# One meeting of the engines per stage, two state recurrences run per feature tile, and a fifth attention term on 128 rows

## The reference

```python
def _hgrn_scan(state, ins, emit):            # chunk by chunk
    def step(S, inp):
        ...
            inter = jnp.einsum('bhtk,bhkv->bhtv', q_c * jnp.exp(g), S)
        ...
        S = (jnp.exp(g_last[:, :, 0, :])[..., None] * S
             + jnp.einsum('bhsk,bhsv->bhkv', k_c * jnp.exp(g_last - g), i_c))
        return S, o

def _rwkv_scan(state, ins, emit):            # token by token
    def step(S, inp):
        sa = jnp.einsum('bhvk,bhk->bhv', S, kk_t)
        S = (S * w_t[:, :, None, :] - sa[..., None] * (kk_t * a_t)[:, :, None, :]
             + v_t[..., None] * k_t[:, :, None, :])
        y = jnp.einsum('bhvk,bhk->bhv', S, inp[5]) if emit else None
        return S, y

def block_attention(qn, qr, kn, kr, v):      # 8 heads, 512 queries, 768 keys
        s = jnp.einsum('bqhd,bkhd->bhqk', qn_b, kn) + jnp.einsum('bqhd,bkd->bhqk', qr_b, kr)
        p = jax.nn.softmax(s.astype(jnp.float32) * scale, axis=-1).astype(v.dtype)
        return jnp.einsum('bhqk,bkhd->bqhd', p, v)
```

## Time and profile before

| what | us |
|---|---|
| median of 3 executions | 2939.48 (2936.7 to 2940.68) |
| the profiled execution | 2932.05 |
| its span, first to last instruction | 2930.1 |
| one pass of the hgrn state stage, first to last work | 9.6 |
| one pass of the rwkv state stage | 24.8 |
| the attention stage | 138 |
| granted TensorE clock, mean | 0.922 |

### The profile page before, as it was taken

The page is one execution under the profiler, slowest core; times in us unless marked ns, Lnnn a source line. Parts: engine busy times, 40 slices in busy tenths (PEclk is TensorE's granted clock), DMA queues, the critical chain, the costliest instruction groups (busy, mean ns, idle before and its releaser), DMA issues. The chain is left out here.

```text
span 2930.1 us, 60098 instructions
## 1 busy us (share of the span) xinstructions
PE 2539.1 (87%) x25174; PEld 2106.5 (72%) x25174; DVE 1476.8 (50%) x2524; ACT 905.7 (31%) x1456; POOL 618.6 (21%) x323
## 2 busy tenths in 40 slices
PE   6956597786977798978988899999997898899998
PEld 3845485684855587768887788888885765688886
DVE  6787777536437764345553444134315455643242
ACT  3243224213124432522124322122214433432232
POOL 0010200110113121200103223222341300544444
PEclk9977697896988899989999999999998999899999
DMA  6521061000005342200004112111214200523232
GB/s 267 180 80 45 14 205 42 3 4 1 4 3 215 138 157 86 72 28 3 3 3 151 51 64 71 58 57 64 71 44 180 77 1 16 200 100 99 89 104 82
DMA packets 63139, 229.31 MB, mean 78 GB/s; under 512 B 6352, under 2 KB 12880, under 8 KB 60880
## 3 DMA queue, kind: packets, MB, share of 16 engines
q1 hardware_dynamic: 62928, 226.22, 22.3%
HBM read 211.52 MB, written 13.63 MB: 77 GB/s over the span
## 5 line engine op out<-in xcount | busy, mean ns | idle before, releaser
L2323 POOL TENSOR_TENSOR b_wl<-b_stage,b_wh 128x1024 fp32r<-128x1024 f32 (+1 forms) x72 | 186.7, 2593 | 477.1 <-ACT b_wh L2319 477.1
L2622 DVE SCALAR_TENSOR_TENSOR f_xr<-f_ps,cols,f_xr 128x511 f32<-128x511 f32 (+1 forms) x132 | 83.2, 658 | 326.2 <-ACT f_xr L2615 326.2
L2454 PE MATMUL f_ps<-h_h,b_wl 128*128 128x256 f32 (+1 forms) x672 | 226.3, 337 | 0.0
L2454 PE MATMUL f_ps<-h_h,b_wh 128*128 128x256 f32 (+1 forms) x672 | 226.1, 336 | 0.0
L2454 PE MATMUL f_ps<-h_l,b_wh 128*128 128x256 f32 (+1 forms) x672 | 225.8, 336 | 0.0
L2319 ACT ACTIVATE b_wh<-b_stage 128x1024 fp32r<-128x1024 f32 (+1 forms) x72 | 81.5, 1131 | 460.3 <-PE f_ps L2454 404.9
L2323 POOL TENSOR_TENSOR c_wl<-c_stage,c_wh 128x1024 fp32r<-128x1024 f32 (+1 forms) x68 | 176.6, 2597 | 221.6 <-ACT c_wh L2319 221.6
L2319 ACT ACTIVATE c_wh<-c_stage 128x1024 fp32r<-128x1024 f32 (+1 forms) x68 | 77.3, 1137 | 266.3 <-PE f_ps L2454 232.8
L2323 POOL TENSOR_TENSOR a_wl<-a_stage,a_wh 128x1024 fp32r<-128x1024 f32 x33 | 85.2, 2581 | 269.2 <-ACT a_wh L2319 269.2
L2454 PEld LDWEIGHTS f_ps<-h_h,b_wh 128*128 128x128 f32 x672 | 127.6, 190 | 13.7
L2454 PEld LDWEIGHTS f_ps<-h_h,b_wl 128*128 128x128 f32 x672 | 127.6, 190 | 13.2
(11 more groups left out here) (716 smaller groups left out, 6698.0 us busy)
## 6 DMA issues: line engine op xcount, KB each, us to landing
b_stage<-in_ffn_up SPq DMA_DIRECT2D x44, 512.0 KB, 3.2
c_stage<-in_ffn_up SPq DMA_DIRECT2D x44, 512.0 KB, 3.2
first_stage<-in_w_in SPq DMA_DIRECT2D x33, 512.0 KB, 3.7
a_stage<-in_ab_w SPq DMA_DIRECT2D x25, 512.0 KB, 3.6
p_hgrn_side_w<-in_ada_w SPq DMA_DIRECT2D x12, 1024.0 KB, 5.0
b_stage<-in_ffn_down SPq DMA_DIRECT2D x16, 704.0 KB, 4.1
c_stage<-in_ffn_down SPq DMA_DIRECT2D x16, 704.0 KB, 4.1
a_in_side_w<-in_ada_w SPq DMA_DIRECT2D x8, 1024.0 KB, 6.4
```

What stands on the lines that cost most here:

```text
L2323: self.nc.gpsimd.tensor_tensor(self.wl[:, slot, :w], self.stage[:, slot, :w], self.wh[:, slot, :w].bitcast(F32), ALU.subtract).then_inc(se ...
L2454: done = self.nc.tensor.matmul(out[s][:, :tn], w, x[:, k, t0:t0 + tn], start=k == 0 and n == 0, stop=k == job.kt - 1 and n == 2)
L2622: nc.vector.scalar_tensor_tensor(out, b[:, :n - 1], self.tap(part, 0, i), out, ALU.mult, ALU.add).then_inc(self.before_ok[part], 1)
```

## The change

`Stage.__exit__` no longer holds the second meeting. The semaphores that a stage gives up are cleared by POOL behind the first meeting as before, but they are kept out of use during the next stage and are handed back only at its end:

```diff
     def __exit__(self, *exc):
         self.mem.close()
         if exc[0] is None:
+            for s in Stage.kept_back:
+                self.nc.release_semaphore(s)
             self.nc.clear_and_free_semaphores(self.sems)
-            self.nc.all_engine_barrier()
+            Stage.kept_back = [self.nc.alloc_semaphore(f"{s.name}_kept_back", num=s.num) for s in self.sems]
```

`hgrn_states` gives each feature tile its own semaphore and its own two banks; decay and addition become one operation:

```diff
-                nc.vector.tensor_tensor(tmp[:, :, :], states[:, c], spread(w["end"][:, :, c], 2, HD), ALU.mult
-                                        ).then_inc(decayed, 1)
-                dve.wait_ge(decayed, n + 2)
-                dve.wait_ge(update, n + 1)
-                nc.vector.tensor_tensor(states[:, order[n + 1]], tmp[:, :, :],
-                                        ps[n % 4][:, :NR * HD].rearrange("p (f v) -> p f v", v=HD), ALU.add
-                                        ).then_inc(added, 1)
+                for f in range(NR):
+                    dve.wait_ge(state_ok[f], n + 1)
+                    dve.wait_ge(update, NR * n + f + 1)
+                    nc.vector.scalar_tensor_tensor(states[:, order[n + 1], f], states[:, c, f], w["end"][:, f, c:c + 1],
+                                                   ps[f][n % 2][:, :HD], ALU.mult, ALU.add).then_inc(state_ok[f], 1)
```

`rwkv_states` gets semaphores `product[f]` and `state_ok[f]`, one bank for each feature tile in place of one for each half, and the readings of y move into the loop:

```diff
+            def step(n, f):
+                c = steps[n]
                 if n:
-                    pe.wait_ge(state_ok, 2 * n)
+                    pe.wait_ge(state_ok[f], n)
+                for e in range(2):
+                    done = nc.tensor.matmul(ps[f][rows64(e), :HD], w["trans"][rows64(e), c, f, :], before(c)[rows64(e), f, :],
+                                            start=True, stop=True)
+                done.then_inc(product[f], 1)
...
+            for n in range(len(steps)):
                 for f in range(NR):
+                    step(n, f)
+                if steps[n] >= CC:
+                    for f in range(NR):
+                        read(steps[n], f)
+            for f in range(NR):
+                pe.wait_ge(state_ok[f], len(steps))
+                read(order[-1], f).then_inc(summed, 1)
...
             for n, c in enumerate(steps):
-                dve.wait_ge(product, n + 1)
-                for e in range(2):
-                    nc.vector.tensor_tensor(states[rows64(e), order[n + 2]], w["gain"][rows64(e), c],
-                                            ps[e][rows64(e), :NR * HD].rearrange("p (f v) -> p f v", v=HD), ALU.add
-                                            ).then_inc(state_ok, 1)
-            dve.wait_ge(summed, 1)
+                for f in range(NR):
+                    dve.wait_ge(product[f], n + 1)
+                    nc.vector.tensor_tensor(states[:, order[n + 2], f], w["gain"][:, c, f], ps[f][:, :HD], ALU.add
+                                            ).then_inc(state_ok[f], 1)
             for f in range(NR):
+                dve.wait_ge(summed, f + 1)
                 nc.vector.tensor_tensor(y[:, f, :], y[:, f, :], yps[f][:, :], ALU.add)
```

In `attention` the fifth term takes the whole of `qr` and `kr_l`, like the fourth:

```diff
-                         (qr[:, h, tok], kr_h[:, :]), (qr[hp, h, tok], kr_l[hp, :]))
+                         (qr[:, h, tok], kr_h[:, :]), (qr[:, h, tok], kr_l[:, :]))
```

More of the change, by code:

```diff
@@ L25 @@
 class Stage:
+    kept_back = ()
     def __init__(self, nc, name):
@@ L832, in hgrn_states @@
         update = st.sem("update")
[L833 to L836, removed]
+        state_ok = [st.sem(f"state{f}") for f in range(NR)]
+        ps = [st.banks(f"ps{f}_", 2) for f in range(NR)]
         block = st.block()
@@ L1528, in rwkv_states @@
     with Stage(nc, f"rwkv{d}_states") as st:
-        product = st.sem("product")
-        state_ok = st.sem("state")
+        product, state_ok = ([st.sem(f"{name}{f}") for f in range(NR)] for name in ("product", "state"))
         summed = st.sem("summed")
-        ps = [st.banks(f"s{e}", 1)[0] for e in range(2)]
+        ps = st.banks("s", NR)
         yps = st.banks("y", NR)
@@ L1542, in _, with read @@
         def _(pe):
-            for n, c in enumerate(steps):
+            def step(n, f):
+                c = steps[n]
                 if n:
-                    pe.wait_ge(state_ok, 2 * n)
-                for f in range(NR):
-                    for e in range(2):
-                        done = nc.tensor.matmul(ps[e][rows64(e), f * HD:(f + 1) * HD], w["trans"][rows64(e), c, f, :],
-                                                before(c)[rows64(e), f, :], start=True, stop=True)
-                done.then_inc(product, 1)
-            pe.wait_ge(state_ok, 2 * len(steps))
-            lates = [c for c in range(CC, NC)]
-            for phase in range(NR):
-                for c in lates:
-                    for e in (1, 0):
-                        f = (phase + e) % NR
-                        done = nc.tensor.matmul(yps[f][rows64(e), (c - CC) * C:(c - CC) * C + C], before(c)[rows64(e), f, :],
-                                                w["rt"][rows64(e), f, (c - CC) * C:(c - CC) * C + C], start=True, stop=True)
-            done.then_inc(summed, 1)
+                    pe.wait_ge(state_ok[f], n)
+                for e in range(2):
+                    done = nc.tensor.matmul(ps[f][rows64(e), :HD], w["trans"][rows64(e), c, f, :], before(c)[rows64(e), f, :],
+                                            start=True, stop=True)
+                done.then_inc(product[f], 1)
+            def read(c, f):
+                for e in range(2):
+                    done = nc.tensor.matmul(yps[f][rows64(e), (c - CC) * C:(c - CC) * C + C], before(c)[rows64(e), f, :],
+                                            w["rt"][rows64(e), f, (c - CC) * C:(c - CC) * C + C], start=True, stop=True)
+                return done
+            for n in range(len(steps)):
+                for f in range(NR):
+                    step(n, f)
+                if steps[n] >= CC:
+                    for f in range(NR):
+                        read(steps[n], f)
+            for f in range(NR):
+                pe.wait_ge(state_ok[f], len(steps))
+                read(order[-1], f).then_inc(summed, 1)
         @block.vector
@@ L4112, in build @@
 def build(nc, d, out):
+    Stage.kept_back = ()
     with ExitStack() as mem:
```

21 lines of the change are left out of this document (8 added, 13 removed).

## The result

The changed kernel takes 2860.81 us (median of four executions, 2856.67 to 2865.28), against 2939.35 for the kernel before on the same chip: a ratio of 0.9732, 95% interval 0.9721 to 0.9744, 78.5 us less. Measured once more beside the last experiments it had 0.9723 (0.9708 to 0.9738). The forecast was 2876.0 with a range from 2861. So the sign and three of four mechanisms held, and the size was 15 us short, just outside the range.

What follows compares the result with a forecast made beforehand. PE, busy 87% of the span, was taken to lose time at 52 stage ends and in handovers with DVE. Savings of 24.4 + 5.8 + 25.4 + 7.9 = 63.5 us from 2939.48 gave 2876.0 us, range 2861 to 2895.

Steps and rivals of the forecast that it cites:

- Term 1: Ends of the 52 stages: without the second all-engine meeting everything behind moves up, saving 24.4 us, at least 20.
- The high end's fear: Stage starts: DVE or PE ready behind the second release need not be ready 0.4 us sooner; meetings' saving then 20 us.
- Term 2: hgrn state stages: three smaller DVE operations replace two, 0.57 us a step for 0.86, saving 5.8 us, bounds 0 to 9.
- Term 3: rwkv state stages: feature tiles follow each other through PE and DVE, 12.1 us for 24.8, saving 25.4, bounds 22 to 31.5.
- Term 4: Attention: fifth term on 128 rows, not 64, saves 0.28 us in each of 28 jobs, 7.9 us, bounds 5.6 to 9.
- One bank for both halves: rwkv state stage: both partition halves in one PSUM bank cost double, that stage's saving is gone, 2901 us; 7%.
- Small operations on DVE don't overlap: State stages: hgrn saving gone, 0.9 us a step against 0.86, rwkv operations stay under PE; 2883 us; 9%.
- The code comes late: Stage starts: engines must fetch their next code, so the meetings' saving is gone, 2900 us, 7%; slower than before, 2%.
- The change doesn't do what it says: Stage ends: the stages still meet twice, only 39.1 us go, 2900 us; 1%.

## Why the prediction was wrong in size, step by step

**Term 1, the meetings (24.4 forecast, 34 measured).** This is the step that failed. What it says of the pauses held: L55 is gone, the first work stands mostly 0.27 to 0.30 us behind the last where it was 0.7, and the pauses shrank by 24.0 us. Wrong was its upper bound: "above it nothing is to be had". I priced the pause and took the stages behind it as given, but the kernels with one meeting have 19 to 34 us less at the half clock outside the pauses, worth 5 to 10 us by the line, and their stages are 5 to 7 us shorter in the traces; the medians say about 10. The range had 4 us for that, put in without a row, and a low end at 2861 that is missed by 0.2 us: near by luck, since it was to be reached by terms 2 and 3 at their best. The high end's fear, a start that is not sooner though the release is, came in only three of the 51 starts (5.2, 255.4 and 2421.2 in the kernel after), where 0.05 to 0.25 us was gained.

**Term 2, hgrn states (5.8 forecast, 5.4 measured).** 0.192 us from one operation to the next where 0.19 was worked out from wider ones, 0.58 a step.

**Term 3, rwkv states (25.4 forecast, 27.0 in the traces, 29.7 by medians).** The steps came as worked out, 0.80, 1.27 and 0.70 us, and the clock rose inside. The stage is 11.3 us and not 12.1, mainly since four of the reading steps were charged at the half clock and only three were, up to 649.5 (the prediction's addends also give 11.9 and not 12.0); in the changed kernel's second recording it took 10.1 and 10.5. A size, within its bounds.

**Term 4, the fifth term (7.9 forecast, 10.7 measured in the stage).** Right in kind, mis-sized beyond its bound of 9. I had read the spacing of the terms up to the start of L3950 and stopped there: 0.09 + 0.20. The second half of the passage out, 0.10 us, lies in the spacing behind the first matmul of L3950 (0.53 us to the next, where the others have 0.43). My doubt ran the wrong way: I allowed that a part of the 0.20 might stay. The stage is 124.7 us and not 130: besides the 2.8 of this term, 1.9 are the clock at its start, and 0.7 are a pause that the 138 us of the earlier trace rows took in.

**The sum.** 24.0 + 5.4 + 27.0 + 10.7 = 67.1 us by the stages' rows, 3.6 over the forecast, and about 10 that the meeting gives beyond its pauses, make 77, against 78.5 measured. Taking the recording's 7.4 us off the median and adding it again was sound.

**The rivals.** *One bank for both halves* is refuted: 24 rows into the same bank take 1.27 us for a step and a reading at a clock of 0.50, 0.053 each, as the alternating banks did; the rule of the Trainium skill (TensorEngine Tiling (Array Packing), Restrictions and Gotchas) that the rival goes back to has no effect here that can be seen. *Small operations on DVE don't overlap* is refuted by 0.192 us between starts at a length of 0.273. The Trainium skill (VectorE: DVE Perf Modes, the TRN2 errata) speaks of a fixed cost of each instruction. It is there all the same: by term 2's 0.067 us for 64 columns, 0.21 us of the length and 0.125 of the spacing are left over. *The code comes late* is refuted by weights that start 0.1 us behind the release. *The change doesn't do what it says* is refuted by the rows of L54 alone.

## What to carry to other kernels

A pause in which all engines stand can be worth more than its length: here 24 us of pauses taken away were about 34 us of time, while 18 us of pauses added were 21. A change that takes them away should be priced with a share for the stages behind. To price a passage between two shapes on PE, read the spacing of starts until it is back to normal, two matmuls beyond the seam and not one. Compare stages of two recordings only with the granted clock beside them, and measure each part of a joint change alone: four single runs showed, within some 8 us, that nothing was owed to their interplay.

## What the runs showed of the hardware

A passage between 128-row and 64-row matmuls costs 0.20 us at a granted clock of 1.00, in two pieces of 0.1: the weight load starts 0.21 us behind the matmul in front, where it else starts with it (2402.19), and the matmul behind the next is late as well. Two passages a job were worth 10.7 us of a 135 us stage, and two more cost some 12.

The same program differs by 15 us from run to run (2926.2 to 2941.5 in 17 executions of the kernel before), and its mean granted clock goes with it in part (correlation -0.65), 0.924 in the fastest and 0.917 to 0.920 in the four slowest.

An unchanged stage of 18 transposes took 2.16 us at a granted clock of 1.00 and 3.67 at 0.57. Over all unchanged stages 1 us at the half clock cost 0.28 us. The Trainium skill (TensorE: Matmul & The Clock Gate, Terms) puts the loss at the share of the clock that is missing, which would be 0.5. These traces don't agree; in the rwkv front stage, at least, PE waits for ACT while its clock is low.
